# Moving ScalarE's exponentials ahead of its copies in the attention stage of a transformer layer

## What is computed

```python
def gqa_block(qi, k_all, v_all):
    s = jnp.einsum('bqkgd,bskd->bkgqs', qi, k_all).astype(jnp.float32) * (HEAD_DIM ** -0.5)
    p = jax.nn.softmax(s, axis=-1).astype(v_all.dtype)
    return jnp.einsum('bkgqs,bskd->bqkgd', p, v_all)

def latent_attention(q, k_lat, v_lat, k_ctx, v_ctx):
    ...
    k_all = jnp.concatenate([k_lat, k_ctx], axis=1)
    v_all = jnp.concatenate([v_lat, v_ctx], axis=1)
    ...
    o = lax.map(lambda qi: gqa_block(qi, k_all, v_all), qb)
```

## Time and profile before

| | us |
|---|---|
| median of 3 runs | 1953.71 |
| range of these runs | 1952.69 to 1958.49 |
| the profiled execution's own time | 1958.15 |
| its span in the profile | 1956.4 |

### The profile page before, as it was taken

The page is one execution under the profiler, slowest core; times in us unless marked ns, Lnnn a source line. Parts: engine busy times, 40 slices in busy tenths (PEclk is TensorE's granted clock), DMA queues, the critical chain, the costliest instruction groups (busy, mean ns, idle before and its releaser), DMA issues.

```text
span 1956.4 us, 27692 instructions
## 1 busy us (share of the span) xinstructions
PE 1811.1 (93%) x8627; PEld 1439.2 (74%) x8627; DVE 1594.1 (81%) x1971; ACT 1285.2 (66%) x1889; POOL 287.0 (15%) x273
## 2 busy tenths in 40 slices
PE   6999989999999998179999999999999999999995
PEld 3777757776777675168888888888888888888884
DVE  5887667777787775769998899899889999988986
ACT  3444366766676665257777777777777777777774
POOL 0233330111011101301110011011001100100113
PEclk8999999999999999589999999999999999999998
DMA  9565671221122111569999999999999999999996
GB/s 377 148 186 155 163 206 42 70 61 48 41 69 60 48 33 39 212 225 414 391 388 364 408 385 371 395 389 378 373 402 390 381 380 389 384 374 397 383 379 244
DMA packets 115203, 515.48 MB, mean 263 GB/s; under 512 B 17184, under 2 KB 43208, under 8 KB 64464
## 3 DMA queue, kind: packets, MB, share of 16 engines
q1 hardware_dynamic: 108960, 492.30, 67.4%
q0 software_dynamic: 4752, 17.30, 3.3%
q10 hardware_dynamic: 1440, 5.24, 0.7%
HBM read 484.86 MB, written 27.33 MB: 262 GB/s over the span
## 4 chain that ended last, share of the span: by engine, by line
PE 56%; DVE 2%; DMA 0%; POOL 0%; issue 0%; ACT 0%; DVEq 0%; ACTq 0%; POOLq 0%
PE banks L1677 36%; PE banks L1702 18%; PE banks L1689 1%; PE banks L1658 1%; DVE topi L1539 1%; DVE top L1537 1%; DVE cand L1540 1%; DVE raw L1632 0%; DMA xe<-h_scratch,icol 0%; POOL fst L1458 0%; DMA out<-raw 0%; ACT banks L1528 0%; POOL fst L1456 0%; DVE ysc L1599 0%; DVE ysc L1639 0%
## 5 line engine op out<-in xcount | busy, mean ns | idle before, releaser
L1571 DVE TENSOR_TENSOR w_lo<-raw,w_hi 128x2048 fp32r<-128x2048 f32 x252 | 565.8, 2286 | 71.3 <-ACT w_hi L1480 71.3
L1480 ACT ACTIVATE w_hi<-raw 128x2048 fp32r<-128x2048 f32 x256 | 470.4, 1920 | 9.6 <-DMA raw<-in_w_exp 9.4
L1677 PE MATMUL banks<-w_hi,x_hi 128*128 128x512 f32 x1024 | 405.2, 396 | 1.4 <-DVE x_lo L1565 1.4
L1677 PE MATMUL banks<-w_hi,x_lo 128*128 128x512 f32 x1024 | 399.6, 390 | 0.0
L1677 PE MATMUL banks<-w_lo,x_hi 128*128 128x512 f32 x1024 | 399.3, 390 | 0.0
L1579 DVE TENSOR_TENSOR d_lo<-raw,d_hi 128x1024 fp32r<-128x1024 f32 x256 | 296.2, 1217 | 1.5 <-ACT d_hi L1502 1.4
L1502 ACT ACTIVATE d_hi<-raw 128x1024 fp32r<-128x1024 f32 x256 | 258.1, 1061 | 39.5 <-DMA raw<-in_w_exp 27.0
L1109 DVE TENSOR_TENSOR ptl<-banks,pth 128x384 fp32r<-128x384 f32 x320 | 177.3, 554 | 76.4 <-ACT pth L1047 72.5
L1047 ACT ACTIVATE pth<-banks 128x384 fp32r<-128x384 f32 x320 | 157.2, 491 | 121.2 <-PE banks L1244 117.9
L1677 PEld LDWEIGHTS banks<-w_hi,x_lo 128*128 128x128 f32 x1024 | 192.6, 188 | 40.8
L1677 PEld LDWEIGHTS banks<-w_hi,x_hi 128*128 128x128 f32 x1024 | 192.7, 188 | 39.7 <-DVE x_lo L1565 1.8
(11 more groups left out here) (217 smaller groups left out, 2685.8 us busy)
## 6 DMA issues: line engine op xcount, KB each, us to landing
raw<-in_w_exp SPq DMA_DIRECT2D x384, 1024.0 KB, 7.6
a_ring<-in_w_mod SPq DMA_DIRECT2D x32, 512.0 KB, 6.9
qt<-q_scratch SPq DMA_DIRECT2D x64, 192.0 KB, 4.7
a_slot<-in_w_mod SPq DMA_DIRECT2D x8, 1024.0 KB, 13.9
a_w_raw<-in_w_in SPq DMA_DIRECT2D x3, 2048.0 KB, 29.6
q_scratch<-a_qst SPq DMA_DIRECT2D x16, 384.0 KB, 4.4
xr<-in_x SPq DMA_DIRECT2D x8, 512.0 KB, 4.1
acc_scratch<-x SPq DMA_DIRECT2D x8, 512.0 KB, 3.2
```

Of the source, the lines that this page charges most:

```text
L1480: act.activation(w_hi[which][c][:, :], raw[which][c][:, :], ACT.Copy).then_inc(s["hi_done"], 1)
L1571: dve.tensor_tensor(w_lo[which][c][:, :], raw[which][c][:, :], w_hi[which][c][:, :].bitcast(F32), ALU.subtract).then_inc(s["lo_done"], 1)
L1677: i = pe.matmul(psum[:, 2 * (j % 2) + which, :], x_[par][:, k, :], w_, start=(k == 0 and w_ is hi and x_ is x_hi), stop=(k == KD - 1 and x ...
```

## The change

ScalarE's loop body is rewritten. In slot 0 it now does the first exponential, the flush copy if there is one, the second exponential, and then the first copy of a turned tile. In slot 1 it does the third exponential ahead of the second copy. Slots 2 and 3 hold copies and the rest of the work. The waits of each instruction, and all other engines' code, are as they were.

```diff
--- before.py
+++ after.py
@@ -1018,9 +1018,10 @@
                 for i in range(NQ):
                     its = items(i, prev, cur)
                     ex = behind(t, i, prev, cur)
-                    for c in range(NCH + 1):
-                        if ex and c < NCH:
-                            tb, h = ex
+                    def exponentials(*chunks):
+
+                        tb, h = ex
+                        for c in chunks:
                             lo, hi = CH[c]
                             if c == 0:
                                 act.wait_ge(s["mn_done"], NQ * tb + h + 1)
@@ -1030,6 +1031,11 @@
                                     act.wait_ge(s["t_done"], KT * (4 * tb + g - 1))
                             act.activation(pr[(h // 3 % 2) * 3 + h % 3][:, lo:hi], psum[:, (NCH * h + c) % 4, 0:hi - lo], ACT.Exp,
                                            bias=mn[:, h, 3:4], scale=-1.0, accum_out=den[:, h, c:c + 1]).then_inc(s["exp_done"], 1)
+                    for c in range(NCH + 1):
+                        if ex and c == 0:
+                            exponentials(0)
+                        if ex and c == 1:
+                            exponentials(2)
                         if c == 0 and i in fl:
                             G = 4 * t + fl[i]
                             act.wait_ge(s["pv_done"], KT * (G + 1))
@@ -1038,6 +1044,8 @@
                                 act.activation(oth[0:HD, :], psum[HD:P, OB, 0:REP * P], ACT.Copy).then_inc(s["oth_done"], 1)
                             else:
                                 act.activation(oth[HD:P, :], psum[0:HD, OB, 0:REP * P], ACT.Copy).then_inc(s["oth_done"], 1)
+                        if ex and c == 0:
+                            exponentials(1)
                         if c < len(its):
                             k = its[c]
                             n = NT * t + k
```

## The result

The changed kernel takes 1986.21 us (median of 4 runs, 1984.96 to 1989.13), the kernel before 1955.91 us beside it (median of 4, 1952.69 to 1958.49). The ratio is 1.0152, with a 95% interval of 1.0138 to 1.0166: 30 us, or 1.5%, slower. The profiled execution took 1984.96 us, its span is 1983.2.

What follows compares the result with a forecast made beforehand. TensorE's fixed order was taken as the bound. Tiles 1 to 7 (23.1), tile 0 (1.3 + 2.7) and the last tile (0.7) sum to 27.8 us; added to 1953.71 this gives 1981.5 us, range 1968 to 1988.

Steps and rivals of the forecast that it cites:

- What bounds the kernel: Attention loop: TensorE, busy 93% of the span, has a fixed order of work; its waits, 4.2 us a tile, lengthen the tile.
- The price of one exponential: On ScalarE, a 512-wide exponential put ahead of the first copy delays that copy by 0.66 us.
- Five places: Steps 0, 3, 8, 9 and 11 of a loop tile each pay 0.66 us: 3.3 a tile, 23.1 over tiles 1 to 7.
- Step 6: Flush step where output projections leave 1.31 us of slack before the last transpose, so the 0.66 us delay costs nothing.
- Steps 1, 2, 4, 5, 7, 10: In loop tiles the copy waits for its transpose anyway, or other TensorE work covers its delay: net 0.
- The third exponential: Put ahead of the second copy, it costs net 0, since the second rest waits for VectorE's queue instead.
- Tile 0: Without output projections: two flush steps cost 1.3 us, three pairs of plain steps 0.9 each, 2.7 us.
- The last pass: The last tile has only the flush of step 0, which pays 0.66 us.
- Faster: Waits for exponentials shrink and the copies' delay stays hidden: at most 6.9 us gained, 1946.8 us; chance 0.07.
- nothing felt: ScalarE has spare time, so gain at the third score matmul and loss at the last transpose cancel: 1953.7 us; chance 0.05.
- partly covered: Flush steps 0, 3, 9 pay; delays of steps 8, 11 and tile 0's plain pairs vanish: 16 us, 1969.7 us; chance 0.08.
- The views foretold: Profile signs: tiles 68.6 us; TensorE's waits for rests about 6, for exponentials 1.2 a tile; VectorE idle 1.8 in flush steps.

Runs made afterwards that it cites:

- e3: Kernel before with the changed order only in steps 0, 3, 6 and 9, the flush steps; ratio 1.0110 to the kernel before.
- e4: Kernel before with the changed order only in steps 8 and 11 of tiles 1 to 7; ratio 1.0037 to the kernel before.
- e6: Changed kernel with the third exponential, like the second, also put ahead of the first copy; 2015.19 us.
- e7: Changed kernel with the second exponential put ahead of the flush copy as well; 1974.83 us.
- e5: Kernel before with the changed order only in steps 1, 2, 4, 5, 7, 10, and in 8 and 11 of tile 0; ratio 1.0011.
- e2: Changed kernel with the second exponential back behind the first copy, the third still ahead of the second copy; 1958.72 us.
- e1: Changed kernel with the third exponential back behind the second copy, the second still ahead of the first copy; 1987.12 us.
- e10: Kernel before with the changed order in step 3 alone; 1963.89 us.
- e8: Kernel before with, in flush steps, second exponential ahead of flush copy and VectorE's second rest ahead of a minimum; norm square earlier in step 7; 1950.55 us.
- e9: Kernel before with second exponential ahead of flush copy in step 3 only, second rest ahead of a minimum in flush steps, norm square earlier in step 7; 1948.63 us.
- e11: The changed kernel run and profiled once more, unaltered; 1984.80 us in one run.

## Why the prediction was right

The forecast was 1981.5 us, slower by 27.8; it is slower by 30.3 between the medians, and the time lies in the range. By its own steps:

- **What bounds the kernel.** TensorE's fixed order of work, by its waits for the rests. Right: the kernels differ in waits alone.
- **The price of one exponential, 0.66 us.** Right: 0.67 in the timeline, 0.66 to 0.68 in each of the five steps that pay.
- **Five places, 3.3 us a tile.** Right, each by itself: after shows them in steps 0, 3, 8, 9 and 11; e3 and e4 take them apart; e6 scales them; e7 takes the one of step 3 away by giving the exponential ScalarE's idle time. Step 6 is covered, as told, though by some 0.94 us (e6) and not by the 1.31 of the forecast.
- **Steps 1, 2, 4, 5, 7, 10: nothing.** Right (e5).
- **The third exponential: nothing.** Right as a part of the change and for the loop. By itself it costs 2.0 us in tile 0 (e2), which the forecast did not see, and which the second exponential's delay covers.
- **Tile 0: flush steps 1.3, plain pairs 2.7.** Measured 1.34 and 2.6. The choice near the upper end, 0.9 a pair, was right (0.86); its reason, that the next exponential waits for a minimum, was not tested.
- **The last pass: 0.66.** Measured 0.5.
- **The rivals.** Faster, nothing felt and partly covered all fall. S2's wait shrank as the rival had it (0.63 to 0.26), and more than that went at T2 and at the first product behind it, which start 0.63 and 0.41 later against their neighbours; T3's own wait, which the forecast had growing too, stayed at 0.62. Steps 8 and 11 pay in full (e4).
- **The views foretold.** Tiles of 68.6: right. VectorE's idle time of 1.8 in flush steps: right. TensorE's waits for exponentials at 1.2 a tile: 1.4. Its waits for rests at about 6: wrong, as the table of waits of the tile from 572.88 to 643.08, to be laid beside the earlier trace rows, says:

```profile
PE banks L1252 <- DVE ptl L1117: 2.7, 7, 0.6
PE banks L1234 <- ACT pr L1032: 1.4, 3, 0.8
PE banks L1192 <- DVE ptl L1117: 1.3, 2, 0.9
PE banks L1292 <- DVE lg L1144: 0.6, 1, 0.6
```

That is 4.0 for rests and 0.6 for the router, in all 6.0 where before it was 4.2: 1.8 more, in tiles that are 3.3 us longer. Another 1.26 us stands as busy time of TensorE (62.38 in the first tile shown above, 61.12 in the earlier trace rows, with the same matmuls), whose ends are modelled: bars that overlapped stand apart, as in step 3 above. The rest lies in gaps that the table leaves out, such as that ahead of step 3's first product. The term of the sum was right, and the view chosen to prove it holds about half of it; the ruler of minima holds all.

What the forecast lacked is the slow tile: 1.5 us in the profile, not in any of its terms. With it, 27.8 becomes the 29.3 that attention shows; that the sum fits so closely is in part luck, since tiles 1 to 7 cost 0.2 more and the other terms 0.3 less than put. The 30.3 of the medians holds what the unprofiled executions did, which no trace shows.

## What to carry to other kernels

Ahead of moving an instruction earlier in an engine's fixed order, look at what it is put ahead of, and follow that one's chain to the bounding engine: an instruction is moved at no cost into idle time that is long enough at that very place (0.63 us in step 3, only 0.40 in steps 0 and 9), and pays its full length where the next one starts at once and is waited for. To price such a move, take a small instruction that occurs once in each step of both kernels and compare step by step; a table of waits showed about half of the loss here, since it counts from ends that are modelled.

## What the runs showed of the hardware

TensorE's granted clock fell inside the loop, which the kernel before does not show in its profile. In the changed kernel, behind the transpose of step 3 that waited 0.61 us (595.97), with 0.25 and 0.47 waited just ahead of it (593.11 and 594.09), the three waits of that step. Windows of one or two microseconds there:

```profile
596.00:597.00 1.00, 1.00 (x6) 1.00 (x7) 0.91 (x3) 0.45 (x2) 0.00 (x0) 0.76 0.00 0
597.00:599.00 2.00, 2.00 (x9) 1.70 (x8) 1.50 (x4) 1.81 (x7) 0.00 (x0) 0.50 0.04 1
599.00:600.00 1.00, 1.00 (x5) 0.70 (x4) 0.56 (x1) 0.52 (x3) 0.00 (x0) 0.53 0.03 3
600.00:601.00 1.00, 1.00 (x8) 0.76 (x7) 0.76 (x2) 0.49 (x1) 0.00 (x0) 1.00 0.60 168
```

The eighth column is the granted clock: 0.50, the lower level of 1.2 GHz, for some 3.4 us, and back to 1.00 with TensorE busy throughout. It costs 70.20 - 68.66 = 1.54 us. Every such fall in the loop of any kernel begins at this place of a tile, at most 0.65 us before or behind the start of T3 of step 3, and all of them are in kernels whose step 3 has the second exponential between the flush copy and the first copy (9 in the 36 tiles profiled of these, none in the 42 of the others):

| kernel | TensorE's waits of over 0.2 us in step 3 | falls in the loop's six periods |
|---|---|---|
| before | 0.63 + 0.62 | 0 |
| after, profiled twice | 0.26 + 0.47 + 0.62 | 1 and 1 |
| e1 (second exponential as after) | | 1 |
| e10 (step 3 as after) | | 1 |
| e3 (step 3 as after) | | 3 |
| e6 | 0.25 + 0.93 + 0.62 | 2 |
| e7 | 0.39 + 0.61 | 0 |
| e2, e4, e5, e8, e9 | | 0 |

The size of the waits alone does not tell the place: in the changed kernel the products of step 9's flush wait 0.90 and 0.40 us within about a microsecond (557.57 and 558.59), and no fall follows them in any tile. Outside the loop the clock fell in every kernel, before included: in the last pass (from 780.2 us before, 804.7 after), and at the start of tile 0 in all but e9 and e11 (251.1 and 248.4 us). Before and after have one such fall each at the start of tile 0, so it is no part of their difference.

So a loss of 0.66 us in one place can bring a second one, more than twice its size, now and then. e10 shows that step 3's order is enough: TensorE's waits in one of its usual tiles add up to 4.2 us, as before, so the rival by which it hangs on the waits of the whole tile falls. In which tiles it falls stays open: I had expected chance, but the second profile of the changed kernel (e11) has it in the same tile as the first, 596 to 599 us, while e1, with the second exponential in the same place, has it one tile later, and e6, with longer waits, has it less often than e3.
